# Local attention with a sink: the value products of a turn as four matmuls on tiles that hold a high and a low half side by side, the halves added outside TensorE, and the masks of the own keys made by GpSimd affine selects

## Chip, core, metric

One NeuronCore of a Trainium2 chip runs the kernel. The metric is the device time of one execution in microseconds, as the median of several runs.

## What is computed

Two transformer blocks follow each other on 512 tokens of width 1024. The change touches one part of the second block, the sliding-window attention with a sink: 16 query heads share 2 key heads of width 64, and a query attends to its own 128-token block up to itself and to the part of the block before that lies within the window of 128.

```python
def sliding_window_sink_attention(q, k, v, sinks, valid):
    ...
    kb, vb = band(k), band(v)          # the block before, then the own block
    ...
    mask = ((diff >= 0) & (diff < WINDOW))[None] & kvalid[:, None, :]
    scores = jnp.where(mask[None, :, None, None], scores, -jnp.inf)
    ...
    probs = jax.nn.softmax(jnp.concatenate([scores, sink], axis=-1), axis=-1)[..., :-1]
    o = jnp.einsum('bnhgqk,bnkhd->bnqhgd', probs.astype(v.dtype), vb)
# second_block
y_sw = (o_sw * jax.nn.silu(sw_z)) @ w_branch_swa[l]
```

A query at place t of its block attends to exactly 128 keys: own keys 0 to t and keys t+1 to 127 of the block before. So one 128x128 tile of probabilities for each head holds both kinds.

## The kernel before

Five engines run programs written out by hand, and semaphores order them. Each engine works strictly in its own order. Exact products come from numbers split into a high part (rounded to the type of the fast matmul, `fp32r`) and a low part (the rest): high by high, high by low and low by high are summed in PSUM.

The local attention runs in 16 turns w = 0 to 15, one for four heads of one block of 128 queries. For one turn:

- TensorE (PE) makes the scores (`window_scores`, L2522). VectorE (DVE) lays the own keys over the keys of the block before (L1906), adds the sink and takes the maximum (`window_max`, L1908). ScalarE (ACT) takes the exponentials (`window_exp`, L1201), VectorE the reciprocals of the sums (`window_norm`, L1914), GpSimd (POOL) multiplies by them (`window_normalised`, L718).
- TensorE transposes the probabilities of four heads into one PSUM bank, 128 keys by 512 (`window_transposed`, L2531). ScalarE copies the bank as the high part into `pwt` (`transposed_hi`), VectorE subtracts it and writes the low part (`transposed_lo`, shown under the helper's line L1651).
- The values are the block before plus a step: o = P·V_before + (P masked to the own keys)·(V_own − V_before). The masked copy of the high part is made by VectorE (L1886), that of the low part by GpSimd (`window_own_low`, L710), each as a product with a 0/1 tile.
- TensorE multiplies (`window_values`, L2543 to L2551): six matmuls of 512 columns into PSUM bank 6. The value tiles `before_hi`, `before_lo`, `step_hi`, `step_lo` hold the same 64 columns twice, so that rows 0 to 63 and rows 64 to 127 of the bank hold the same sums; the output of an even head is read from the first, that of an odd head from the second.
- VectorE multiplies the bank by half the gate (`window_out`, L1898, two instructions of 64x256), ScalarE makes the high part of the result (`window_out_hi`), GpSimd the low part (`window_out_lo`, L696).

Around it TensorE interleaves, for each pass w of its loop, the scores of turn w+2, some steps of the gate projections (`merge_gate`, three matmuls a step, under L1982 to L1984), the transposes of turn w, and the values of turn w−1. In passes 15 and 16 a branch product of 12 matmuls stands in the place of the gate steps. GpSimd also makes the low part of two weight slabs in six pieces (`part_low`, L703) in passes 3, 4, 6, 7, 11 and 12; whole slabs before and after are under L632. VectorE makes the low part of slab 21 in pass 14 (L1651). `pwt` is one buffer before the change: ScalarE may not overwrite it before the six matmuls of the last turn have ended (`swo_done`).

Of the kernel before, what the change touches and what calls it, by code (L numbers as in the profile page):

```python
# [12 lines left out]
P = 128  # L13
SEQ, D = 512, 1024
NT, KT = SEQ // P, D // P
HD = 64
# [87 lines left out]
def build(nc, a, out):  # L104
    with ExitStack() as ctx:
# [43 lines left out]
        step_hi = sb("step_hi", [P, NT, 2, 2, HD], F32R, at[0] - 4 * KB)  # L149
# [79 lines left out]
        step_lo = sb("step_lo", [P, NT, 2, 2, HD], F32R)  # L229
        r_tokm = region(4 * KB)  # L230
        before_hi = sb("before_hi", [P, NT, 2, 2, HD], F32R, r_tokm)
# [7 lines left out]
        at[0] = tok_start + 5 * KB  # L239
        before_lo = sb("before_lo", [P, NT, 2, 2, HD], F32R)  # L240
        pwt = sb("pwt", [P, 2, 2, SEQ], F32R)
# [159 lines left out]
        sqp_done = sem("sqp_done")  # L401
# [30 lines left out]
        ymain_done = sem("ymain_done")  # L432
# [14 lines left out]
        sw_exp = sem("sw_exp")  # L447
        pw_ready = sem("pw_ready")
# [124 lines left out]
        def _(pool):  # L573
# [103 lines left out]
            def values_low(lo, v, hi, copy_):  # L677

                return pool.tensor_tensor(lo[:, :, :, copy_, :], v.rearrange("p t (g d) -> p t g d", g=2),
                                          hi[:, :, :, copy_, :].bitcast(F32), ALU.subtract)  # L680

            pool.wait_ge(vw_hi, 1)
            for copy_ in range(2):
                values_low(step_lo, v_step[:], step_hi, copy_).then_inc(vw_lo, 1)
            pool.wait_ge(vw_hi, 2)
            pool.wait_ge(tw_done, 10)
            for copy_ in range(2):
                values_low(before_lo[:, 0:1], insert_dim(v_meta[:], 1, 1), before_hi[:, 0:1], copy_)
                values_low(before_lo[:, 1:], tokw[:, 0:3, 1152:1280], before_hi[:, 1:], copy_).then_inc(vw_lo, 1)
# [17 lines left out]
            def window_own_low(w):  # L707

                pool.wait_ge(tw_lo, 10 + w + 1)
                pool.tensor_tensor(by_head(pwt[:, 1, 1, :]), by_head(pwt[:, 1, 0, :].bitcast(F32)),  # L710
                                   insert_dim(own_keys.bitcast(F32), 1, 4), ALU.mult).then_inc(window_own_lo, 1)
# [11 lines left out]
            for w in range(16):  # L723
                window_own_low(w)
# [32 lines left out]
        def _(act):  # L757
# [386 lines left out]
            def values_high(hi, v):  # L1144

                for copy_ in range(2):
                    last = copy(hi[:, :, :, copy_, :], v.rearrange("p t (g d) -> p t g d", g=2))
                return last

            for half in range(2):  # L1150
                split2(11 + 2 * half)
                if half == 1:
                    act.wait_ge(v_step_ready, 2)
                    values_high(step_hi, v_step[:]).then_inc(vw_hi, 1)
# [30 lines left out]
            act.wait_ge(vw_lo, 2)  # L1185
            values_high(before_hi[:, 0:1], insert_dim(v_meta[:], 1, 1))
            values_high(before_hi[:, 1:], tokw[:, 0:3, 1152:1280]).then_inc(vw_hi, 1)
# [39 lines left out]
            def window_out_hi(w):  # L1227

                n, u = turn_of(w)
                act.wait_ge(swo_read, w + 1)  # L1230
                copy(qw[:, 4 * u:4 * u + 4:2, n * P:n * P + P], yw[:, w % 2]).then_inc(yw_hi, 1)

            merge_tanh(0)
            for w in range(16):
                transposed_hi(w)
                if w == 14:
                    split2(21)
# [8 lines left out]
                if w + 1 in GATE_ENDS:  # L1246
                    merge_tanh(1 + GATE_ENDS.index(w + 1))
            window_out_hi(15)
# [33 lines left out]
        def _(dve):  # L1282
# [1423 lines left out]
```

## Time and profile before

| | us |
|---|---|
| median of 3 runs (966.72 to 967.11) | 966.81 |
| the profiled execution, time | 967.21 |
| the profiled execution, span of the trace | 965.4 |
| PE busy | 948.9 (98%) |
| PEld (weight load) busy | 798.0 (83%) |
| DVE busy | 632.7 (66%) |
| ACT busy | 465.0 (48%) |
| POOL busy | 262.5 (27%) |

The span lies within the time of the execution; the difference is 1.8 us at its ends. Busy shares are those of the whole program; the 16 turns take about 75 us of it.

### The profile page before, as it was taken

The numbers are of one execution on the slowest core, as the hardware profiler recorded it, in microseconds if no ns is written. First come the engines' busy times: TensorE is split into PE (matmuls) and PEld (weight loads), VectorE is DVE, ScalarE is ACT, GpSimd is POOL, SyncE is SP. The second block draws the span as 40 slices with busy tenths as digits, with TensorE's granted clock in tenths as the row PEclk, the third lists the DMA queues.
The fourth block names the chain that finished last, engine by engine and source line by source line (L and its number), as shares of the span: only waits on it lengthen the run. The fifth ranks groups of instructions, "written<-read, shape, count | busy, mean of one in ns | idle before, by whom it ended". The sixth has DMA issues, their size and how long they took to land.

```text
span 965.4 us, 12758 instructions
## 1 busy us (share of the span) xinstructions
PE 948.9 (98%) x4782; PEld 798.0 (83%) x4782; DVE 632.7 (66%) x914; ACT 465.0 (48%) x844; POOL 262.5 (27%) x190
## 2 busy tenths in 40 slices
PE   7999999999999999999999999999999999999997
PEld 6988888888888888888888888988888887888886
DVE  5677787946787687864755887699547775312314
ACT  5435665725444565634447778523555652221212
POOL 2226000003235000002253010151358884315141
PEclk9999999999999999999999999999999999999999
DMA  9232201132422201143222111122220113232312
GB/s 299 90 112 76 96 23 44 44 131 79 144 88 88 93 19 63 45 131 83 88 88 88 43 45 44 45 88 88 87 88 22 45 43 109 88 105 93 131 44 87
DMA packets 64189, 79.84 MB, mean 83 GB/s; under 512 B 5744, under 2 KB 47856, under 8 KB 64128
## 3 DMA queue, kind: packets, MB, share of 16 engines
q1 hardware_dynamic: 62224, 76.13, 24.6%
q10 hardware_dynamic: 1904, 2.88, 0.9%
q8 instruction: 40, 0.66, 0.3%
q14 instruction: 21, 0.17, 0.1%
HBM read 76.91 MB, written 2.10 MB: 82 GB/s over the span
## 4 chain that ended last, share of the span: by engine, by line
PE 41%; issue 40%; POOL 8%; ACT 6%; DVE 4%; DMA 1%; POOLq 0%; ACTq 0%; DVEq 0%
PE ps L1982 12%; PE ps L1983 11%; PE ps L1984 11%; POOL small L604 2%; PE ps L2522 1%; POOL t L614 1%; POOL sq L614 1%; DVE sp L1745 1%; ACT spr L1016 1%; DMA x<-in_x 1%; POOL small L591 1%; DVE wlo L1651 1%; ACT qsb L1016 1%; PE ps L2531 1%; POOL small L593 1%
## 5 line engine op out<-in xcount | busy, mean ns | idle before, releaser
L632 POOL TENSOR_TENSOR wlo<-raw,whi 128x2048 fp32r<-128x2048 f32 (+1 forms) x23 | 101.1, 4395 | 184.8 <-ACT whi L1010 175.4
L1982 PE MATMUL ps<-whi,hhi 128*128 128x512 f32 (+1 forms) x320 | 115.7, 362 | 1.1 <-issue 0.4
L1984 PE MATMUL ps<-whi,hlo 128*128 128x512 f32 (+1 forms) x320 | 114.5, 358 | 0.0
L1983 PE MATMUL ps<-wlo,hhi 128*128 128x512 f32 (+1 forms) x320 | 114.4, 357 | 0.0
L1982 PE MATMUL ps<-hhi,whi 128*128 128x512 f32 x288 | 113.5, 394 | 0.6 <-POOL wlo L703 0.6
L1984 PE MATMUL ps<-hhi,wlo 128*128 128x512 f32 x288 | 112.4, 390 | 0.0
L1983 PE MATMUL ps<-hlo,whi 128*128 128x512 f32 x288 | 112.2, 390 | 0.0
L1010 ACT ACTIVATE whi<-raw 128x2048 fp32r<-128x2048 f32 (+1 forms) x29 | 52.9, 1826 | 84.4 <-PE ps L1984 75.9
L1320 DVE TENSOR_TENSOR wlo<-raw,whi 128x2048 fp32r<-128x2048 f32 (+1 forms) x29 | 63.6, 2192 | 37.4 <-ACT whi L773 30.9
L773 ACT ACTIVATE whi<-raw 128x2048 fp32r<-128x2048 f32 (+1 forms) x29 | 52.1, 1798 | 69.4 <-PE ps L1984 69.4
L2039 PE MATMUL ps<-hhi,whi 128*128 128x512 f32 x192 | 76.8, 400 | 0.0
L2041 PE MATMUL ps<-hhi,wlo 128*128 128x512 f32 x192 | 75.1, 391 | 0.0
L2040 PE MATMUL ps<-hlo,whi 128*128 128x512 f32 x192 | 74.8, 390 | 0.0
L1651 DVE TENSOR_TENSOR wlo<-raw,whi 128x2048 fp32r<-128x2048 f32 x10 | 23.6, 2357 | 72.9 <-ACT whi L1010 72.7
L1982 PEld LDWEIGHTS ps<-whi,hhi 128*128 128x128 f32 x320 | 60.5, 189 | 11.3 <-issue 2.3
L618 POOL TENSOR_TENSOR small<-small 128x4 f32<-128x4 f32 x2 | 0.4, 201 | 253.1 <-ACT junk L971 253.1
L1984 PEld LDWEIGHTS ps<-whi,hlo 128*128 128x128 f32 x320 | 60.5, 189 | 8.9
L1983 PEld LDWEIGHTS ps<-wlo,hhi 128*128 128x128 f32 x320 | 60.5, 189 | 8.3
L1982 PEld LDWEIGHTS ps<-hhi,whi 128*128 128x128 f32 x288 | 54.1, 188 | 11.8 <-POOL wlo L703 0.8
L1984 PEld LDWEIGHTS ps<-hhi,wlo 128*128 128x128 f32 x288 | 54.1, 188 | 11.6
L1983 PEld LDWEIGHTS ps<-hlo,whi 128*128 128x128 f32 x288 | 54.1, 188 | 10.3
L898 ACT ACTIVATE prob<-ps,small 128x512 f32<-128x512 f32 x64 | 43.4, 685 | 25.0 <-DVE small L1525 24.9
(339 smaller groups left out, 2266.2 us busy)
## 6 DMA issues: line engine op xcount, KB each, us to landing
raw<-in_w_in SPq DMA_DIRECT2D x42, 1024.0 KB, 5.3
raw<-in_w_out SPq DMA_DIRECT2D x12, 1024.0 KB, 5.0
raw<-in_w_in SPq DMA_DIRECT2D x10, 512.0 KB, 4.0
raw<-in_w_branch_swa SPq DMA_DIRECT2D x4, 1024.0 KB, 5.0
raw<-in_w_branch_sb SPq DMA_DIRECT2D x4, 512.0 KB, 3.4
x<-in_x ACTq DMA_DIRECT2D x3, 512.0 KB, 6.6
out<-x SPq DMA_DIRECT2D x3, 512.0 KB, 2.6
ws<-in_spatial_w SPq DMA_DIRECT2D x2, 512.0 KB, 6.6
```

The source lines that it names most:

```text
L632: pool.tensor_tensor(wlo[s][:, 0:n, :], raw[s][:, 0:n, :], whi[s][:, 0:n, :].bitcast(F32), ALU.subtract).then_inc(slab_split, 1)
L773: act.activation(whi[s][:, :, 0:w], raw[s][:, :, 0:w], ACT.Copy).then_inc(whi_done, 1)
L898: act.activation(prob[:, t, :], ps[:, n % 3, :], ACT.Exp, bias=nmax[:, m:m + 1], accum_out=pair_sums(psum_e, h // 2)[:, m:m + 1]).then_inc ...
L1010: act.activation(whi[s][:, 0:n, :], raw[s][:, 0:n, :], ACT.Copy).then_inc(whi_done, 1)
L1320: dve.tensor_tensor(wlo[s][:, :, 0:w], raw[s][:, :, 0:w], whi[s][:, :, 0:w].bitcast(F32), ALU.subtract).then_inc(slab_split, 1)
L1651: return dve.tensor_tensor(lo, src, hi.bitcast(F32), ALU.subtract)
L1982: pe.matmul(out_ap, lhsT=lhi(k), rhs=rhi(k), start=first and k == 0, stop=False, skip_group_check=True)
L1983: pe.matmul(out_ap, lhsT=lhi(k), rhs=rlo(k), start=False, stop=False, skip_group_check=True)
L1984: m = pe.matmul(out_ap, lhsT=llo(k), rhs=rhi(k), start=False, stop=last and k == n - 1, skip_group_check=True)
L2039: pe.matmul(ps[:, bank, :], lhsT=wh, rhs=hhi[:, k, :], start=k == 0, stop=False)
L2040: pe.matmul(ps[:, bank, :], lhsT=wh, rhs=hlo[:, k, :], start=False, stop=False)
L2041: m = pe.matmul(ps[:, bank, :], lhsT=wl, rhs=hhi[:, k, :], start=False, stop=k == KT - 1)
```

## The change

The tiles `before` and `step` now hold the high part in columns 0 to 63 and the low part in columns 64 to 127 (for each of the two key heads). One matmul with such a tile gives the product with the high part in PSUM rows 0 to 63 and that with the low part in rows 64 to 127; four matmuls make a turn: `before` and `step`, each with the high and the low part of the probabilities. The two halves of the bank have to be added. For even heads the addend stands in rows 64 to 127, for odd heads in rows 0 to 63: ScalarE copies it across into a tile `other` (`window_other_half`), VectorE adds it to the half that stays, and a third VectorE instruction of 128x256 multiplies by the gate. Both masked copies are now made on GpSimd (`window_own`) by `affine_select`, which takes the element where query − key ≥ 0 and writes zero elsewhere. `pwt` has two buffers. On VectorE the order of `transposed_lo` and `window_out` in a pass is turned round. The preparation of the value tiles writes each part once, not twice.

```diff
-        pwt = sb("pwt", [P, 2, 2, SEQ], F32R)
+        other = sb("other", [P, 2, P])
+        pwt = sb("pwt", [P, 2, 2, 2, SEQ], F32R)
...
+            def window_own(w, part):
+
+                pool.wait_ge((tw_hi, tw_lo)[part], 10 + w + 1)
+                place = lambda own: by_head(pwt[:, w % 2, part, own, :])
+                pool.affine_select(place(1), place(0).bitcast(F32), [[0, 4], [1, P]], ALU.is_ge, 0.0, base=0,
+                                   channel_multiplier=-1).then_inc((window_own_hi, window_own_lo)[part], 1)
...
             for w in range(16):
-                window_own_low(w)
+                window_own(w, 0)
+                window_own(w, 1)
...
             def transposed_hi(w):
                 act.wait_ge(tw_done, 10 + w + 1)
+                if w >= 2:
+                    act.wait_ge(swo_done, w - 1)
+                copy(pwt[:, w % 2, 0, 0, :], ps[:, 4 + w % 2, :]).then_inc(tw_hi, 1)
+
+            def window_other_half(w):
+
+                act.wait_ge(swo_done, w + 1)
                 if w:
-                    act.wait_ge(swo_done, w)
-                copy(pwt[:, 0, 0, :], ps[:, 4 + w % 2, :]).then_inc(tw_hi, 1)
+                    act.wait_ge(swo_read, w)
+                for e in range(2):
+                    r, o = slice(64 * e, 64 * e + 64), slice(64 - 64 * e, P - 64 * e)
+                    last = copy(other[r], ps[o, 6, :].rearrange("p (c e n) -> p c e n", c=2, e=2)[:, :, e, :])
+                last.then_inc(other_done, 1)
...
             for w in range(16):
                 transposed_hi(w)
+                if w:
+                    window_other_half(w - 1)
...
             def transposed_lo(w):
 
                 dve.wait_ge(tw_hi, 10 + w + 1)
-                low(pwt[:, 1, 0, :], ps[:, 4 + w % 2, :], pwt[:, 0, 0, :]).then_inc(tw_lo, 1)
-                dve.tensor_tensor(by_head(pwt[:, 0, 1, :]), by_head(pwt[:, 0, 0, :].bitcast(F32)),
-                                  insert_dim(own_keys.bitcast(F32), 1, 4), ALU.mult).then_inc(window_own_hi, 1)
+                p = pwt[:, w % 2]
+                low(p[:, 1, 0, :], ps[:, 4 + w % 2, :], p[:, 0, 0, :]).then_inc(tw_lo, 1)
...
-                    last = dve.scalar_tensor_tensor(yw[r, w % 2], o, 0.5, gate_sw[r, 2 * u:2 * u + 2, n * P:n * P + P],
-                                                    ALU.mult, ALU.mult)
+                    last = dve.tensor_tensor(yw[r, w % 2], o, other[r], ALU.add)
                 last.then_inc(swo_read, 1)
+                dve.wait_ge(swo_read, w + 1)
+                dve.scalar_tensor_tensor(yw[:, w % 2], yw[:, w % 2], 0.5, gate_sw[:, 2 * u:2 * u + 2, n * P:n * P + P],
+                                         ALU.mult, ALU.mult).then_inc(window_gated, 1)
...
-                pe.matmul(ps[:, 6, :], lhsT=v(before_hi), rhs=pwt[:, 0, 0, :], start=True, stop=False)
-                pe.matmul(ps[:, 6, :], lhsT=v(before_lo), rhs=pwt[:, 0, 0, :], start=False, stop=False)
+                pe.matmul(ps[:, 6, :], lhsT=v(before), rhs=p[:, 0, 0, :], start=True, stop=False)
                 pe.wait_ge(tw_lo, 10 + w + 1)
-                pe.matmul(ps[:, 6, :], lhsT=v(before_hi), rhs=pwt[:, 1, 0, :], start=False, stop=False)
+                pe.matmul(ps[:, 6, :], lhsT=v(before), rhs=p[:, 1, 0, :], start=False, stop=False)
                 pe.wait_ge(window_own_hi, w + 1)
-                pe.matmul(ps[:, 6, :], lhsT=v(step_hi), rhs=pwt[:, 0, 1, :], start=False, stop=False)
-                pe.matmul(ps[:, 6, :], lhsT=v(step_lo), rhs=pwt[:, 0, 1, :], start=False, stop=False)
+                pe.matmul(ps[:, 6, :], lhsT=v(step), rhs=p[:, 0, 1, :], start=False, stop=False)
                 pe.wait_ge(window_own_lo, w + 1)
-                pe.matmul(ps[:, 6, :], lhsT=v(step_hi), rhs=pwt[:, 1, 1, :], start=False, stop=True).then_inc(swo_done, 1)
+                pe.matmul(ps[:, 6, :], lhsT=v(step), rhs=p[:, 1, 1, :], start=False, stop=True).then_inc(swo_done, 1)
```

GpSimd's order at the start of the turns, before. The first row is the low part of slab 18, and the rows on `pwt` are the masked low parts of turns 0, 1 and 2.

```order
L632 TENSOR_TENSOR wlo_55<-raw_51,whi_53 128x2048 [waits whi_done]
L710 TENSOR_TENSOR pwt<-pwt,consts_r 128x512 [waits tw_lo]
L718 TENSOR_TENSOR pw<-pw,small_99 128x4x128 [waits inv_ready]
L710 TENSOR_TENSOR pwt<-pwt,consts_r 128x512 [waits tw_lo]
L696 TENSOR_TENSOR qw<-yw,qw 128x2x128 [waits yw_hi]
```

The same place after the change (its line numbers are the changed file's: L629 is the slab's low part, L706 `window_own`, L714 `window_normalised`, L691 `window_out_lo`).

```order
L629 TENSOR_TENSOR wlo_55<-raw_51,whi_53 128x2048 [waits whi_done]
L706 ISA
L706 AFFINE_SELECT pwt<-pwt 128x512 [waits tw_hi]
L706 AFFINE_SELECT pwt<-pwt 128x512 [waits tw_lo]
L714 TENSOR_TENSOR pw<-pw,small_99 128x4x128 [waits inv_ready]
L706 AFFINE_SELECT pwt<-pwt 128x512 [waits tw_hi]
L706 AFFINE_SELECT pwt<-pwt 128x512 [waits tw_lo]
L691 TENSOR_TENSOR qw<-yw,qw 128x2x128 [waits yw_hi]
```

VectorE's order in one turn, before: low part, masked high part, `window_max`, `window_norm`, and then the output of the turn.

```order
L1651 TENSOR_TENSOR pwt<-ps,pwt 128x512 [waits tw_hi]
L1886 TENSOR_TENSOR pwt<-pwt,consts_r 128x512
L1906 COPY_PREDICATED ps<-consts_r,ps 128x4x128 [waits sw_scored]
L1907 COPY ps<-sink 128x4 [waits dch]
L1908 TENSOR_REDUCE small_99<-ps 128x4 [waits dch]
L1914 RECIPROCAL small_99<-small_99 128x4 [waits sw_exp]
L1898 SCALAR_TENSOR_TENSOR yw<-ps,gate_sw 64x256 [waits swo_done]
L1898 SCALAR_TENSOR_TENSOR yw<-ps,gate_sw 64x256
```

After (L1659 is the low part, L1905 the addition of the halves, L1908 the gating):

```order
L1659 TENSOR_TENSOR pwt<-ps,pwt 128x512 [waits tw_hi]
L1905 TENSOR_TENSOR yw<-ps,other 64x256 [waits other_done]
L1905 TENSOR_TENSOR yw<-ps,other 64x256
L1908 SCALAR_TENSOR_TENSOR yw<-yw,gate_sw 128x256 [waits swo_read]
L1915 COPY_PREDICATED ps<-consts_r,ps 128x4x128 [waits sw_scored]
```

The masked high part is gone from VectorE, a gating instruction of its own has come, and the output of a turn now stands between the low part and `window_max`.

## Rows read from the trace of the kernel before

**Rows 1.** busy time by stretches: PE, PEld, DVE, ACT, POOL, then clock, DMA

```profile
729.00:802.00 73.00, 72.04 (x392) 60.51 (x391) 56.98 (x117) 39.98 (x146) 60.32 (x51) 1.00 0.14 44
...
850.00:900.00 50.00, 50.00 (x222) 41.43 (x221) 8.93 (x11) 11.73 (x13) 14.46 (x4) 1.00 0.32 102
```

**Rows 2.** waits of TensorE from 730 us on: us, times, longest

```profile
PE ps L1982 <- POOL wlo L703: 0.6, 1, 0.6
PE ps L2551 <- POOL pwt L710: 0.4, 1, 0.4
```

**Rows 3.** TensorE in order of time, values of turn 1: start, length

```profile
734.25 0.60 PE L2531 MATMUL ps<-ident,pw 128*128 128x128 f32 x4
734.61 0.48 PE L2543 MATMUL ps<-pwt,before_hi 128*128 128x512 f32 x1
734.92 0.40 PE L2544 MATMUL ps<-pwt,before_lo 128*128 128x512 f32 x1
...
735.85 0.39 PE L2551 MATMUL ps<-pwt,step_hi 128*128 128x512 f32 x1
```

**Rows 4.** GpSimd by line and shape: busy us, mean ns, idle before

```profile
L710 POOL TENSOR_TENSOR pwt<-pwt,consts_r 128x512 fp32r<-128x512 f32 x16 | 26.9, 1682 | 11.7 <-DVE pwt L1651 11.7
L718 POOL TENSOR_TENSOR pw<-pw,small 128x512 f32<-128x512 f32 x16 | 16.6, 1040 | 1.0 <-DVE small L1914 1.0
L696 POOL TENSOR_TENSOR qw<-yw,qw 128x256 fp32r<-128x256 f32 x16 | 13.8, 861 | 1.3 <-ACT qw L1016 1.3
L703 POOL TENSOR_TENSOR wlo<-raw,whi 128x512 fp32r<-128x512 f32 x6 | 7.7, 1288 | 0.0
L649 POOL CAST whi<-raw 128x2048 fp32r<-128x2048 f32 x4 | 7.6, 1900 | 70.8 <-DVE spr L1651 70.8
```

**Rows 5.** GpSimd and VectorE in order of time, turns 0 and 1

```profile
723.87 4.61 POOL L632 TENSOR_TENSOR wlo<-raw,whi 128x2048 fp32r<-128x2048 f32 x1 [0.55 <-ACT whi L1010]
727.85 1.19 DVE L1886 TENSOR_TENSOR pwt<-pwt,consts_r 128x512 fp32r<-128x512 f32 x1
728.44 1.74 POOL L710 TENSOR_TENSOR pwt<-pwt,consts_r 128x512 fp32r<-128x512 f32 x1
...
732.93 0.68 DVE L1886 TENSOR_TENSOR pwt<-pwt,consts_r 128x512 fp32r<-128x512 f32 x1
733.10 1.67 POOL L710 TENSOR_TENSOR pwt<-pwt,consts_r 128x512 fp32r<-128x512 f32 x1 [1.32 <-DVE pwt L1651]
```

**Rows 6.** VectorE by line and shape, 715 to 805 us

```profile
L1898 DVE SCALAR_TENSOR_TENSOR yw<-ps,gate_sw 64x256 f32<-64x256 f32 x32 | 13.5, 422 | 14.3 <-PE ps L2551 14.0
L1886 DVE TENSOR_TENSOR pwt<-pwt,consts_r 128x512 fp32r<-128x512 f32 x16 | 12.6, 790 | 0.0
L1908 DVE TENSOR_REDUCE small<-ps 128x4 f32<-128x516 f32 x16 | 11.1, 695 | 0.5
L1651 DVE TENSOR_TENSOR pwt<-ps,pwt 128x512 fp32r<-128x512 f32 x16 | 11.1, 692 | 1.4 <-ACT pwt L1016 0.9
```

**Rows 7.** ScalarE by line, then waits, 710 to 810 us

```profile
L1016 ACT ACTIVATE qw<-yw 128x256 fp32r<-128x256 f32 x16 | 6.9, 430 | 4.8 <-DVE yw L1898 4.6
...
ACT pwt L1016 <- PE ps L2551: 26.0, 15, 2.9
POOL pwt L710 <- DVE pwt L1651: 11.7, 13, 1.6
```

**Rows 8.** TensorE, VectorE and GpSimd in order of time, last turns

```profile
791.62 0.49 PE L2551 MATMUL ps<-pwt,step_hi 128*128 128x512 f32 x1
794.64 2.98 DVE L1651 TENSOR_TENSOR wlo<-raw,whi 128x2048 fp32r<-128x2048 f32 x1 [0.32 <-ACT whi L1010]
795.43 2.78 POOL L696 TENSOR_TENSOR qw<-yw,qw 128x256 fp32r<-128x256 f32 x1
```

**Rows 9.** GpSimd in order of time, the first microseconds

```profile
0.85 0.10 POOL L576 MEMSET small<- 128x8 f32 x1
5.56 0.19 POOL L582 TENSOR_TENSOR small<-small 128x1 f32<-128x1 f32 x1 [4.60 <-ACT junk L797]
```

More of the change, by code:

```diff
@@ L228, in build @@
         gate_sw = sb("gate_sw", [P, 8, SEQ])
-        step_lo = sb("step_lo", [P, NT, 2, 2, HD], F32R)
         r_tokm = region(4 * KB)
-        before_hi = sb("before_hi", [P, NT, 2, 2, HD], F32R, r_tokm)
+        before = sb("before", [P, NT, 2, 2, HD], F32R, r_tokm)
         tokm = sb("tokm", [META, 1, 256], F32, r_tokm)
@@ L676, in _, with values_low @@
                         .then_inc(v_step_ready, 1)
-            def values_low(lo, v, hi, copy_):
-                return pool.tensor_tensor(lo[:, :, :, copy_, :], v.rearrange("p t (g d) -> p t g d", g=2),
-                                          hi[:, :, :, copy_, :].bitcast(F32), ALU.subtract)
+            def values_low(tile, v):
+                return pool.tensor_tensor(tile[:, :, :, 1, :], v.rearrange("p t (g d) -> p t g d", g=2),
+                                          tile[:, :, :, 0, :].bitcast(F32), ALU.subtract)
             pool.wait_ge(vw_hi, 1)
-            for copy_ in range(2):
-                values_low(step_lo, v_step[:], step_hi, copy_).then_inc(vw_lo, 1)
+            values_low(step, v_step[:]).then_inc(vw_lo, 1)
             pool.wait_ge(vw_hi, 2)
             pool.wait_ge(tw_done, 10)
-            for copy_ in range(2):
-                values_low(before_lo[:, 0:1], insert_dim(v_meta[:], 1, 1), before_hi[:, 0:1], copy_)
-                values_low(before_lo[:, 1:], tokw[:, 0:3, 1152:1280], before_hi[:, 1:], copy_).then_inc(vw_lo, 1)
+            values_low(before[:, 0:1], insert_dim(v_meta[:], 1, 1))
+            values_low(before[:, 1:], tokw[:, 0:3, 1152:1280]).then_inc(vw_lo, 1)
             def window_out_lo(w):
@@ L1144, in values_high @@
             def values_high(hi, v):
-                for copy_ in range(2):
-                    last = copy(hi[:, :, :, copy_, :], v.rearrange("p t (g d) -> p t g d", g=2))
-                return last
+                return copy(hi[:, :, :, 0, :], v.rearrange("p t (g d) -> p t g d", g=2))
             for half in range(2):
@@ L1184, in _ @@
             act.wait_ge(rope2_done, 5)
-            act.wait_ge(vw_lo, 2)
-            values_high(before_hi[:, 0:1], insert_dim(v_meta[:], 1, 1))
-            values_high(before_hi[:, 1:], tokw[:, 0:3, 1152:1280]).then_inc(vw_hi, 1)
+            act.wait_ge(vw_lo, 1)
+            values_high(before[:, 0:1], insert_dim(v_meta[:], 1, 1))
+            values_high(before[:, 1:], tokw[:, 0:3, 1152:1280]).then_inc(vw_hi, 1)
             def transposed_hi(w):
                 act.wait_ge(tw_done, 10 + w + 1)
-                if w:
-                    act.wait_ge(swo_done, w)
-                copy(pwt[:, 0, 0, :], ps[:, 4 + w % 2, :]).then_inc(tw_hi, 1)
+                if w >= 2:
[3 more added lines that the diff above has]
+                act.wait_ge(swo_done, w + 1)
+                if w:
+                    act.wait_ge(swo_read, w)
[3 more added lines that the diff above has]
+                last.then_inc(other_done, 1)
             def window_exp(w):
@@ L1229, in window_out_hi @@
                 n, u = turn_of(w)
-                act.wait_ge(swo_read, w + 1)
+                act.wait_ge(window_gated, w + 1)
                 copy(qw[:, 4 * u:4 * u + 4:2, n * P:n * P + P], yw[:, w % 2]).then_inc(yw_hi, 1)
@@ L1921, in _ @@
             for w in range(16):
+                transposed_lo(w)
                 if w:
                     window_out(w - 1)
-                transposed_lo(w)
                 if w == 14:
```

19 lines of the change are left out of this document (7 added, 12 removed).

## Prediction

> **What bounds the kernel now.** I read the page's table of engines first: TensorE is busy for 98% of the span, and since matmuls overlap there, I went on to what it waits for. From 730 us to the end it waits twice, 0.6 and 0.4 us, both times for GpSimd [rows 2]; the stretches behind the turns show it busy without a gap [rows 1]. So a microsecond that TensorE saves in the turns arrives at the end, and so does one that it loses. In the turns the other engines are not far behind: of 73 us GpSimd is busy for 60.3 and VectorE for 57.0, ScalarE for 40.0 [rows 1]. GpSimd's 60.3 already is 83%, and the change gives it work while it shortens the time in which the work must be done. That is the question of this case.
>
> **What TensorE saves.** In a row of value products the starts are (735.85 − 734.92) / 4 = 0.23 us apart [rows 3]; the first takes 0.31 and stays. Two of six go in each turn: 2 × 0.23 × 16 = 7.4 us, the most that can be gained.
>
> **What VectorE and ScalarE get.** VectorE loses the masked copy (0.79 mean, 0.68 undisturbed) and gains a gating of 256 columns; its nearest row is the old output instruction with as many columns, 0.42 [rows 5, 6]. The two additions cost what the two old instructions did. So VectorE gets shorter by 0.26 a turn, unless it is held (next part). ScalarE gets two copies of 64x256; a copy of 128x256 takes 0.43 [rows 7], so at most 0.86 a turn. It waited 26.0 us in 15 turns for the last matmul of the turn before, because `pwt` was one buffer [rows 7]; that wait goes, and the copies, which wait for the same matmul, take its place. Queued behind them are `window_exp` and, on VectorE behind the additions, `window_max` (0.70 for its reduction [rows 6]), whose scores TensorE made a whole pass earlier. I cost this at nothing on the path; if that cover were gone, it would be the 0.86 × 16 = 14 us of the copies at worst. The preparation of the value tiles gets shorter on ScalarE and GpSimd, but ahead of the turns GpSimd next waits for others, at last for the slab whose low part starts at 723.87 with 0.55 us of idle time ahead of it [rows 5]: nothing gained.
>
> **What GpSimd gets.** Here a hold has to be read first. VectorE's masked copy reads two tiles of SBUF. The one at 727.85 takes 1.19 instead of 0.68: GpSimd's slab runs until 728.48, and the copy ends at 729.04. GpSimd's next, begun 728.44, ends at 730.18, 1.14 us after that. The one at 733.10 takes 1.67, and VectorE's copy runs until 733.61: again 1.16 of its own [rows 5]. In the last turns a VectorE subtraction of two SBUF tiles takes 2.98 and a GpSimd one beside it 2.78, where 0.86 is that line's mean [rows 4, 8]. So while one of the two engines runs such an instruction, the other is held until its end. The Trainium skill says this too (GPSIMD Engine Reference, Specifications: shared SBUF interfaces, contention with VectorE instructions that have two SBUF inputs); the rows agree. The masked copy held GpSimd for about 0.5 a turn; that goes. The new gating reads `yw` and `gate_sw`, both SBUF, so it holds GpSimd for 0.42, and waits itself for what GpSimd is doing.
>
> Let a be the time of one select. Until TensorE's last value matmul of turn 13, GpSimd must finish, from 728.48 on: 14 pairs of selects (28a), 12 low parts of the output at 0.73 (the line's 13.8 us less the 2.78, over 15), 13 normalisations at 1.04, 6 slab pieces at 1.29, and 13 holds of 0.42 [rows 4, 6, 8]: 28a + 8.8 + 13.5 + 7.7 + 5.5 = 28a + 35.5. I add 2 us, an estimate for idle time in the first turns, where it has not fallen behind (before it waited 11.7 in 13 turns [rows 7]). TensorE came to that matmul at 791.62 [rows 8]; without 14 × 0.46 = 6.4 us it would be there at 785.2, which leaves GpSimd 56.7 us. It is late from a = (56.7 − 37.5) / 28 = 0.69 on, and each 0.1 us more costs 2.8 us.
>
> No row shows a select. From below: the cast, one operand, takes 1.90 for 2048 columns, which is 0.48 for 512 [rows 4]. From above: the product that makes the same masked tile with two operands, 1.67 as it stands, 1.15 without the hold [rows 4, 5]. Nothing excludes more than that, since a select must also make its condition for each element. I take 0.95, nearer to the product, whose tile and four rows of 128 it shares. Then GpSimd needs 26.6 + 37.5 = 64.1, and TensorE waits 64.1 − 56.7 = 7.4 us, at the third and fourth value matmul: all of the saving.
>
> The Trainium skill prices single-input instructions on GpSimd as roughly at line rate (GPSIMD Engine Reference, When to use GPSIMD), which would be 512 cycles at 1.2 GHz, an estimate of 0.43 us, and so no lateness; the same page (Performance versus the Vector engine) puts branching on data at about 12 cycles an element, 5.1 us here. The sum goes by neither.
>
> **The `ISA` row.** The reload of the library stands between the slab and the first select, with TensorE's values of turn 0 due 1.3 us later. Its like at the start ran in an idle stretch of 4.60 us that ended when ScalarE's result came [rows 9], so it takes between 0 and 4.6. Since nothing shows that it filled the stretch, I take 1.2. The skill puts the first call after loading code at about 6 us (GPSIMD Engine Reference, Instruction dispatch); the 4.60 of the stretch is less, so here the rows and the page differ.
>
> **The last turns.** In turns 14 and 15 VectorE's 2.98 us now stands ahead of `transposed_lo` of turn 15, and two selects instead of one product follow; TensorE already waited 0.4 there [rows 2, 8]. An estimate from these rows: 1.0 more.
>
> **Sum**: −7.4 + 7.4 + 1.2 + 1.0 = +2.2 us. On the profiled execution 967.21 + 2.2 = 969.4; the median shown is 0.4 below that execution, so 969.0.
>
> **The rivals.**
> 1. Forecast: the select takes 0.8 to 1.15, the reload little. GpSimd becomes the bound of the turns. With 0.8: −7.4 + 3.2 + 2.2 = −2.0; with 1.15: −7.4 + 13.0 + 2.2 = +7.8. Its own range is 965 to 975. Chance 0.37.
> 2. Faster: the select is near the cast, 0.5 to 0.75. At 0.54 GpSimd needs 15.1 + 37.5 = 52.6, under 56.7. A turn with a slab piece takes it 1.08 + 0.73 + 1.04 + 1.29 + 0.42 = 4.6, more than TensorE's, so about 1 us stays, and 0.5 for the reload: −7.4 + 1.5 = −5.9, 960.9. It decides the sign at a = (56.7 + 7.4 − 2.2 − 37.5) / 28 = 0.87. For it speaks that only one operand is read. Chance 0.28.
> 3. The reload is dear: 3 to 4.6 us, during which TensorE stands in turn 0, at a select of 0.8: −2.0 − 1.2 + 4 = +0.8, at 0.95 +5.0; 967.6 to 972. For it: an instruction in front of the first select that nothing needed before. Against it: the same library is loaded already. Chance 0.20.
> 4. The select is dearer than the product. At 1.67: 46.8 + 37.5 − 56.7 = 27.6, less 7.4, and 2.2: +22.4, 989. The skill's branching rule would make it 28 × 5.1 + 37.5 − 56.7 = 124 of waiting; the slow end of this case, a chance of 0.02 within it. Chance 0.15.
>
> **Numbers.** A measurement of this kernel tells about 0.2%, 1.9 us, from no change. Faster: most of rival 2 (0.26) and the lower end of the forecast (0.05). Same: 0.13 of the forecast, 0.05 of rival 3, 0.02 of rival 2: 0.20. Slower: the rest, 0.49. Range for 8 in 10: from rival 2's 961 to 982, which is a select of 1.45; beyond it lie the faster tip of rival 2 and most of rival 4.
>
> **What the profile after would show.** Right: 64 matmuls of values; the selects near 0.95 without a hold; GpSimd nearly without idle time from 729 to 785; TensorE waiting at the values for the selects, some 7 us in all; the gating on VectorE longer than 0.42 where it meets GpSimd. Wrong: selects of 0.6 and a GpSimd that still waits for VectorE (rival 2); a gap of several us ahead of the first select only (rival 3); or TensorE waiting for `other` or `swo_read`, which I cost at nothing.

## The result and the profile after

The changed kernel takes 960.38 us (median of 4 runs, 960.18 to 960.69) where the kernel before takes 966.76 beside it: a ratio of 0.9932, interval 0.9921 to 0.9944. It is faster by 6.4 us, 0.66%. The forecast of 969.0 had the wrong sign and the time lies below its range; the time is close to the second rival's 960.9, the one with a cheap select. The profiled execution took 960.69 us, against 967.21 before: 6.5 less.

GpSimd by line and shape, 715 to 806 us, in the changed kernel (busy us, mean ns, idle time before; to be laid beside [rows 4]):

```profile
L706 POOL TENSOR_SCALAR_AFFINE_SELECT pwt<-pwt 128x512 fp32r<-128x512 f32 x32 | 21.2, 684 | 0.1
L714 POOL TENSOR_TENSOR pw<-pw,small 128x512 f32<-128x512 f32 x16 | 16.7, 1044 | 4.3 <-DVE small L1923 4.1
L691 POOL TENSOR_TENSOR qw<-yw,qw 128x256 fp32r<-128x256 f32 x16 | 13.5, 846 | 12.1 <-ACT qw L1013 12.1
L698 POOL TENSOR_TENSOR wlo<-raw,whi 128x512 fp32r<-128x512 f32 x6 | 7.7, 1289 | 0.0
```

32 selects take 21.2 us, where 16 products took 26.9. GpSimd is idle for some 16 us in this window, waiting for ScalarE's copy (12.1) and VectorE's inverse (4.1). The same engine in order of time: the selects of turns 0, 2 and 3, then of 12, 14 and 15:

```profile
724.03 4.61 POOL L629 TENSOR_TENSOR wlo<-raw,whi 128x2048 fp32r<-128x2048 f32 x1 [0.55 <-ACT whi L1007]
728.67 1.23 POOL L706 TENSOR_SCALAR_AFFINE_SELECT pwt<-pwt 128x512 fp32r<-128x512 f32 x2
...
736.06 1.22 POOL L706 TENSOR_SCALAR_AFFINE_SELECT pwt<-pwt 128x512 fp32r<-128x512 f32 x2
...
740.43 1.41 POOL L706 TENSOR_SCALAR_AFFINE_SELECT pwt<-pwt 128x512 fp32r<-128x512 f32 x2
...
779.48 1.29 POOL L698 TENSOR_TENSOR wlo<-raw,whi 128x512 fp32r<-128x512 f32 x1
780.73 1.41 POOL L706 TENSOR_SCALAR_AFFINE_SELECT pwt<-pwt 128x512 fp32r<-128x512 f32 x2
...
788.19 1.22 POOL L706 TENSOR_SCALAR_AFFINE_SELECT pwt<-pwt 128x512 fp32r<-128x512 f32 x2
790.23 2.54 POOL L691 TENSOR_TENSOR qw<-yw,qw 128x256 fp32r<-128x256 f32 x1 [0.81 <-ACT qw L1013]
792.72 1.22 POOL L706 TENSOR_SCALAR_AFFINE_SELECT pwt<-pwt 128x512 fp32r<-128x512 f32 x2
```

A pair of selects takes 1.22, so one takes 0.61; where VectorE's gating meets the pair, it takes 1.41. The reload of the library stands between 724.03 + 4.61 = 728.64 and 728.67: a gap of 0.03 us, where the product before began 0.04 us ahead of its slab's end [rows 5].

The waits of TensorE and its weight load from 729 us on (us in total, times, longest), beside [rows 2]:

```profile
PEld ps L1991 <- POOL wlo L698: 1.3, 1, 1.3
...
PE ps L1991 <- POOL wlo L698: 1.1, 1, 1.1
PEld ps L2559 <- POOL pwt L706: 1.0, 3, 0.4
PEld ps L2557 <- POOL pwt L706: 0.7, 1, 0.7
...
PE ps L2557 <- POOL pwt L706: 0.3, 1, 0.3
```

And TensorE in order of time: the values of turns 0, 12 and 15 (the last):

```profile
729.91 0.48 PE L2553 MATMUL ps<-pwt,before 128*128 128x512 f32 x1
...
730.69 0.39 PE L2559 MATMUL ps<-pwt,step 128*128 128x512 f32 x1
...
780.94 0.39 PE L2555 MATMUL ps<-pwt,before 128*128 128x512 f32 x1
781.60 0.51 PE L2557 MATMUL ps<-pwt,step 128*128 128x512 f32 x1 [0.28 <-POOL pwt L706]
782.19 0.50 PE L2559 MATMUL ps<-pwt,step 128*128 128x512 f32 x1
...
794.58 0.39 PE L2559 MATMUL ps<-pwt,step 128*128 128x512 f32 x1
```

In turn 12 the last three values start 0.66 and 0.59 apart instead of 0.23: 0.8 us lost behind two selects that came late. That is the second wait of the changed kernel, the first being 1.1 for the slab's last low part. The last value of turn 15 starts at 800.90 before and at 794.58 after:

```profile
800.13 0.40 PE L2549 MATMUL ps<-pwt,step_lo 128*128 128x512 f32 x1
800.90 0.50 PE L2551 MATMUL ps<-pwt,step_hi 128*128 128x512 f32 x1 [0.37 <-POOL pwt L710]
```

(of the kernel before, the same view). The difference of 6.32 can be added up from starts. From the first value of turn 0 (729.77 before, 729.91 after) to the last of turn 15 the kernel before takes 71.13 and the changed one 64.67, 6.46 less; 0.14 goes because turn 0 begins later. In 11 of the 15 steps from a turn's first value to the next turn's the changed kernel is shorter by 0.44 to 0.47, 5.06 in all: that is the two matmuls. The rest, in us:

| stretch | before | after | gained | what stands in it |
|---|---|---|---|---|
| turn 7 to turn 8 | 5.01 | 5.01 | 0.00 | the wait for the slab's last low part, 0.6 before, 1.1 after |
| turn 12 to turn 13 | 4.83 | 5.01 | −0.18 | after: 0.78 lost behind late selects |
| turn 13 to turn 14 | 4.65 | 4.38 | 0.27 | after: 0.17 lost at the last value |
| turn 14 to turn 15 | 4.19 | 3.78 | 0.41 | |
| turn 15, first to last value | 1.68 | 0.78 | 0.90 | before: a gap of 0.77 ahead of the very last value |

5.06 + 0.00 − 0.18 + 0.27 + 0.41 + 0.90 = 6.46. Without its wait the step from turn 7 to turn 8 takes 3.71 in the kernel with earlier pieces below, so the wait costs the changed kernel 1.30; with the selects alone it takes 4.30, so it cost the kernel before 0.71. Behind the last value nothing changes: 164.5 us to the end of the trace before, 164.4 after.

Both waits name GpSimd, but the chain of work that ended last (the profile's critical chain, start and length in us) begins further back. For the slab's last part, and then for the late selects of turn 12:

```profile
752.21 0.38 ACT other L1013
...
752.61 1.51 ACT pw L1206 x8
...
761.40 1.23 POOL wlo L698
```

```profile
774.86 0.39 ACT other L1013
...
776.16 0.51 DVE yw L1908
...
779.52 1.25 POOL wlo L698
```

The first goes from the last value of turn 5 through ScalarE's copy of the other half, the exponentials, a piece of the slab's high part and `window_out_hi`, to GpSimd, which then has no gap until the slab's last low part at 761.40. The second goes from the last value of turn 10 through that copy, the additions, the gating and `window_max` to GpSimd's normalisation, the slab piece and the selects. So the copies, which the change adds to ScalarE, are on the path at both places, and the additions at the second.

### The profile page after: what moved, and what is told of

Same layout as the page of the kernel before. It is cut to its first block, busy times and chain, and to the rows that moved or that the text cites. A ratio compares the mean times of both kernels' runs of the same rounds, so it can differ in the third digit from the quotient of the medians.

```text
span 959.0 us, 12753 instructions
## 1 busy us (share of the span) xinstructions
PE 941.1 (98%) x4750; PEld 791.2 (83%) x4750; DVE 629.9 (66%) x914; ACT 477.2 (50%) x873; POOL 253.4 (26%) x203
## 4 chain that ended last, share of the span: by engine, by line
issue 40%; PE 40%; POOL 8%; ACT 5%; DVE 4%; DMA 1%; POOLq 0%; ACTq 0%; DVEq 0%
PE ps L1991 12%; PE ps L1993 11%; PE ps L1992 11%; POOL small L601 2%; DMA x<-in_x 1%; PE ps L2531 1%; POOL t L611 1%; POOL sq L611 1%; DVE sp L1753 1%; ACT spr L1013 1%; POOL small L588 1%; ACT qsb L1013 1%; DVE wlo L1659 1%; PE ps L2267 1%; ACT sp L1077 1%
## 5 line engine op out<-in xcount | busy, mean ns | idle before, releaser
L629 POOL TENSOR_TENSOR wlo<-raw,whi 128x2048 fp32r<-128x2048 f32 (+1 forms) x23 | 101.1, 4396 | 183.5 <-ACT whi L1007 174.1
L1659 DVE TENSOR_TENSOR wlo<-raw,whi 128x2048 fp32r<-128x2048 f32 x10 | 22.9, 2287 | 72.8 <-ACT whi L1007 72.5
```

The costliest lines, as they stand in the source:

```text
L629: pool.tensor_tensor(wlo[s][:, 0:n, :], raw[s][:, 0:n, :], whi[s][:, 0:n, :].bitcast(F32), ALU.subtract).then_inc(slab_split, 1)
L1659: return dve.tensor_tensor(lo, src, hi.bitcast(F32), ALU.subtract)
```

## The experiments

Each was measured beside the kernel before, whose medians in the three sets of runs were 967.13, 966.94 and 966.90 us.

**What the two matmuls bring.** The second value product is issued three times, so that there are six again (the same product added twice more; the output is another).

```
-                pe.matmul(ps[:, 6, :], lhsT=v(before), rhs=p[:, 1, 0, :], start=False, stop=False)
+                for _ in range(3):
+                    pe.matmul(ps[:, 6, :], lhsT=v(before), rhs=p[:, 1, 0, :], start=False, stop=False)
```

> The changed kernel with the second value matmul (before x low part) issued three times, so that a turn has six matmuls again; the output is not the reference's. Theory A, the gain is TensorE's two matmuls a turn and nothing else: 32 x 0.23 = 7.4 us come back, less some waiting for GpSimd that they hide, 966 to 968 us. Rival B, the gain is from the second buffer of the probabilities and from lighter work on VectorE: the time stays under 963.

966.27 us, ratio 0.9992 (0.9983 to 1.0002). Theory A: with six matmuls everything else that the change does comes to no difference that can be told. The 5.9 us to the changed kernel are the matmuls: 7.4 less what TensorE then waits for selects, which it didn't here (its one wait is 1.0 for the slab).

**The masks as products.**

```
-                pool.affine_select(place(1), place(0).bitcast(F32), [[0, 4], [1, P]], ALU.is_ge, 0.0, base=0,
-                                   channel_multiplier=-1).then_inc((window_own_hi, window_own_lo)[part], 1)
+                pool.tensor_tensor(place(1), place(0).bitcast(F32), insert_dim(own_keys.bitcast(F32), 1, 4),
+                                   ALU.mult).then_inc((window_own_hi, window_own_lo)[part], 1)
```

> The changed kernel with both masked copies on GpSimd as products with the 0/1 tile, in the place of the selects. Theory A, the forecast's account of GpSimd is right and only the price of the select was off: at 1.15 us for a product GpSimd needs 28 x 1.15 + 37.5 = 69.7 us where TensorE leaves it 56.7, so 13 us of waiting come on top of the changed kernel's 960.4, 973. Rival B, GpSimd has room that the account does not see: 965 or less.

971.93 us, ratio 1.0052 (1.0035 to 1.0069), 1 us under Theory A's 973. GpSimd by line, 715 to 806 us, then TensorE's waits from 700 us on:

```profile
L706 POOL TENSOR_TENSOR pwt<-pwt,consts_r 128x512 fp32r<-128x512 f32 x32 | 43.0, 1364 | 0.0
```

```profile
PE ps L2559 <- POOL pwt L706: 6.0, 9, 0.9
PE ps L1991 <- POOL wlo L698: 1.5, 1, 1.5
PE ps L2557 <- POOL pwt L706: 1.4, 3, 0.7
PE ps L2553 <- DVE yw L1905: 0.5, 1, 0.5
```

This is the profile that the prediction described (GpSimd without idle time before its masks, TensorE waiting some 7 us for them at the third and fourth value) at twice the select's price: what it said of this mechanism is right, and some 11 us hang on the kind of instruction alone.

**The masks where they were**: the high part's product on VectorE, the low part's on GpSimd, the rest as changed.

```
+                dve.tensor_tensor(by_head(p[:, 0, 1, :]), by_head(p[:, 0, 0, :].bitcast(F32)),
+                                  insert_dim(own_keys.bitcast(F32), 1, 4), ALU.mult).then_inc(window_own_hi, 1)
...
-                window_own(w, 0)
                 window_own(w, 1)
```

> The changed kernel with the masks made as before the change: the high part as a product on VectorE, the low part as a product on GpSimd. Theory A, VectorE would become the bound: its turn is 0.61 + 0.61 + 0.89 + 0.45 + 1.54 + 0.20 = 4.3 us where TensorE's mean turn is 4.07, and each product there and the gating meet GpSimd's holds: 965 to 970, slower than the changed kernel by 5 or more. Rival B, the four matmuls gain without the selects: 960 to 962.

969.51 us (968.21 to 970.48), ratio 1.0025 (1.0014 to 1.0036): Theory A. The two matmuls, bought with the halves, are worth nothing if the masks stay. In the traced execution, one of the fastest (968.28), TensorE waits 3.2 us for the product on GpSimd, 2.0 for VectorE's additions and 1.9 for the slab, and GpSimd's low parts of the slab are held (mean 1.73 instead of 1.29). The eight executions fall into two groups by the mean clock that TensorE was granted: 968.21 to 968.42 at 0.999 of the full clock, and 969.42 to 970.48 at 0.996 or 0.997. So some 1.2 us of the 2.4 that the median lies above the kernel before go with a lower clock. Masks as products don't pay in either place; whether one product on VectorE beside one select on GpSimd would, was not run.

**One buffer for the turned weights.**

```
-                if w >= 2:
-                    act.wait_ge(swo_done, w - 1)
-                copy(pwt[:, w % 2, 0, 0, :], ps[:, 4 + w % 2, :]).then_inc(tw_hi, 1)
+                if w:
+                    act.wait_ge(swo_done, w)
+                copy(pwt[:, 0, 0, 0, :], ps[:, 4 + w % 2, :]).then_inc(tw_hi, 1)
...
```

> The changed kernel with a single buffer of the transposed probabilities, so that ScalarE waits for the last matmul of the turn before, as before the change. Theory A, the two buffers hide a part: masks start about 0.9 us later in a turn, and TensorE waits in the turns with slab pieces, 1 to 2 us in all, 961.5 to 962.5. Rival B, the buffer is what makes the gain: 965 or more.

963.59 us (963.40 to 965.01), ratio 0.9967 (0.9953 to 0.9982): 3.2 above the changed kernel, between the theories. The traced execution is a slow one of the five, 964.64. In it ScalarE's wait for the last value is back (13.8 us in 14 turns), and TensorE waits 0.8 + 0.2 for selects, 0.5 for the additions and 1.6 for the slab. Behind that last wait it also loses its clock. Busy times from 764 to 766 us (the third number from the right is the granted clock), then a matmul of the gate:

```profile
764.00:766.00 2.00, 2.00 (x6) 1.47 (x5) 1.90 (x5) 0.94 (x4) 1.63 (x3) 0.50 0.61 185
```

```profile
764.76 0.63 PE L1991 MATMUL ps<-hhi,whi 128*128 128x512 f32 x1
```

The granted clock is 0.50 from 764 to 767 us (1.2 GHz, the lower of its two levels), and the next matmul starts 0.42 later instead of 0.23. From the end of the wait to the first value of turn 8 it takes 3.16 where the changed kernel takes 1.85, and another 0.29 is lost by turn 9: 1.6 us by the clock, of the 3.95 that this execution lies above the traced one of the changed kernel. The changed kernel's wait of 1.1 us at the same place left the clock at 1.00, and so did one of 1.9 in the traced kernel with the masks as before.

**One select more in each turn**, into a tile that nobody reads:

```
+                if part == 0:
+                    pool.wait_ge(spare_done, w)
+                    pool.affine_select(by_head(spare[:]), place(0).bitcast(F32), [[0, 4], [1, P]], ALU.is_ge, 0.0, base=0,
+                                       channel_multiplier=-1).then_inc(spare_done, 1)
```

> The changed kernel, with one select more in each turn: the high part's select is made twice, first into a tile that nobody reads. GpSimd gets 16 x 0.61 = 9.8 us of work more. It asks what headroom GpSimd has, that is from what price of a select on TensorE would be late. Theory A (the account of the prediction with the select as measured): GpSimd must finish 42 selects and 35.5 us of other work in the 56.7 us up to turn 13, and 42 x 0.61 + 35.5 + 2 = 63.1, so TensorE waits about 6 us more at the third and fourth value matmul: 966 to 967. Theory B (the account's other terms are too high, since the selects hardly hold VectorE and are hardly held by it; GpSimd was idle for some 16 us in the changed kernel's turns): most of the 9.8 us goes into idle time and TensorE waits only 1 to 4 us more: 961.5 to 964.5. Theory C (GpSimd far from the path): under 961.

964.31 us (963.92 to 965.96), ratio 0.9975 (0.9965 to 0.9986): Theory B, near its upper edge.

**Every select twice**, the same lines for both parts:

> The changed kernel with every select made twice, first into a tile that nobody reads, which prices a select at 2 x 0.61 = 1.22 us. This is the upper end of the prediction's first case. Theory A (the account of the prediction): 28 x 1.22 + 37.5 = 71.7 against 56.7 us, so TensorE waits 15 us: 975. Theory B (the account's other terms are some 4 to 5 us too high): the slope of 28 us for each us of price stands once GpSimd has no idle time left, and the time is 969 to 972, that is, from the one extra select of the kernel before it another 7 to 8.5 us, all of it as TensorE's waiting for selects. If instead the second extra select costs under 5 us, GpSimd is still not the bound of the turns even at 1.22.

970.68 us (969.63 to 971.52), ratio 1.0039 (1.0024 to 1.0054): the time is Theory B's, but it lies 6.4 us above the kernel with one extra, less than the 7 to 8.5 expected. One turn of GpSimd in it, in order of time:

```profile
743.65 0.74 POOL L693 TENSOR_TENSOR qw<-yw,qw 128x256 fp32r<-128x256 f32 x1
744.35 1.05 POOL L719 TENSOR_TENSOR pw<-pw,small 128x512 f32<-128x512 f32 x1
745.35 1.30 POOL L700 TENSOR_TENSOR wlo<-raw,whi 128x512 fp32r<-128x512 f32 x1
746.59 0.83 POOL L709 TENSOR_SCALAR_AFFINE_SELECT spare<-pwt 128x512 fp32r<-128x512 f32 x1
747.38 0.63 POOL L711 TENSOR_SCALAR_AFFINE_SELECT pwt<-pwt 128x512 fp32r<-128x512 f32 x1
747.97 0.63 POOL L709 TENSOR_SCALAR_AFFINE_SELECT spare<-pwt 128x512 fp32r<-128x512 f32 x1
748.55 0.63 POOL L711 TENSOR_SCALAR_AFFINE_SELECT pwt<-pwt 128x512 fp32r<-128x512 f32 x1
749.16 0.73 POOL L693 TENSOR_TENSOR qw<-yw,qw 128x256 fp32r<-128x256 f32 x1
```

From start to start the turn takes 749.16 − 743.65 = 5.51. By the prediction's prices it would be 0.73 + 1.04 + 1.29 + 0.42 + 4 × 0.61 = 5.92. Two things make it shorter: each instruction starts 0.02 to 0.06 before the row of the one ahead ends (seven times, 0.30 in all), and the hold costs the held select 0.2 (0.83 against 0.63), not the gating's 0.42; against them the lengths themselves are 0.11 above the prices. Together 0.41. Over 13 turns, some of them without a slab piece, that is 4 to 5 us, about what the account's 975 was above the measured 970.7.

**The selects without the rest**: the kernel before, both masks as selects, VectorE's masked copy gone, six matmuls and one buffer.

```
...
+                for part in range(2):
+                    pool.wait_ge((tw_hi, tw_lo)[part], 10 + w + 1)
+                    pool.affine_select(by_head(pwt[:, part, 1, :]), by_head(pwt[:, part, 0, :].bitcast(F32)), ...)
...
-                dve.tensor_tensor(by_head(pwt[:, 0, 1, :]), by_head(pwt[:, 0, 0, :].bitcast(F32)),
-                                  insert_dim(own_keys.bitcast(F32), 1, 4), ALU.mult).then_inc(window_own_hi, 1)
```

> The kernel before with one part of the change: both masked copies made as selects on GpSimd, VectorE's masked copy gone; six value matmuls, one pwt and the old output instructions stay. Theory A (TensorE was hardly waiting for masks, 1.0 us in all the turns of the kernel before, so moving them gains at most that): 965.8 to 967.2, no change that can be told. Theory B (the masks were what bounded the turns of the kernel before, by the chain from the transposes through VectorE's masked copy to the values): 962 to 964.5, and then part of the gain is the masks' and not that of the two matmuls.

965.34 us, ratio 0.9983 (0.9974 to 0.9992): 1.6 us faster, 0.5 below Theory A's band and 0.8 above Theory B's. TensorE waits for nothing from 700 to 800 us; what went are the waits of [rows 2], with the weight load's share of them: 0.71 ahead of turn 8, 0.39 in turns 12 and 13, and 0.54 ahead of the very last value. So the selects are worth more than the 1.0 us of waits that TensorE's own rows show.

**The slab's pieces a turn earlier.**

```
-GATE_SLAB_HI, GATE_SLAB_LOW = [3, 4, 6, 7], [4, 5, 7, 8]
+GATE_SLAB_HI, GATE_SLAB_LOW = [3, 4, 5, 6], [4, 5, 6, 7]
```

> The changed kernel with another place for the pieces of the output gate's slab: ScalarE's high parts at turns 3, 4, 5, 6 instead of 3, 4, 6, 7 and GpSimd's low parts at 4, 5, 6, 7 instead of 4, 5, 7, 8. The first scores-sized matmul of the gate on this slab waits 1.1 us for the last low part at 762.7 us, plus some at the weight load. Theory A (the piece simply comes a turn late): the wait goes and nothing is late in its place, 958.8 to 959.6. Theory B (GpSimd has four turns with a piece in a row, each 4.3 to 4.6 us against TensorE's 4.1, so its selects fall behind): TensorE waits for the selects in turns 6 and 7 instead, 960 to 961.5.

958.94 us, ratio 0.9917 (0.9904 to 0.9931). Once more, with the changed kernel on the same chip:

> The changed kernel as it is, once more, on the same chip as the two variants that follow: 960.2 to 960.7 as before. It is the measure for them.

> The kernel with the slab's pieces a turn earlier, beside the changed kernel on the same chip. Theory A (the 1.1 us wait for the last low piece is gone and was on the path): 1.1 to 1.7 us under the changed kernel beside it. Theory B (the 958.94 measured before was the chip's): less than 0.5 us under it.

960.67 (960.33 to 960.75) and 959.10 us (958.99 to 959.51). The runs don't overlap: 1.6 us faster than the changed kernel, Theory A. TensorE's only wait there is 0.3, at L2557 in turn 12; four full turns in a row are no trouble, since GpSimd has slack right before and behind them (0.55 and 0.60 us of idle time) and takes 4.44 us for such a turn, where TensorE's take 4.29 on average there, too little to fall behind by in four turns.

**The next slab's pieces apart.**

```
-BRANCH_HI, BRANCH_LOW = [9, 10], [12, 13]
+BRANCH_HI, BRANCH_LOW = [9, 10], [10, 12]
```

> The kernel with the early pieces, and GpSimd's two low pieces of the next slab at turns 10 and 12 instead of 12 and 13, so that they no longer stand in two turns one behind the other, where TensorE waited 0.3 us for a select and its weight load 0.7. Theory A (that wait was GpSimd's lateness in two full turns): it goes, 958.3 to 958.8. Theory B (one full turn is enough to make a select late, since the piece stands right ahead of it): 958.8 to 959.3, the wait only moves.

959.03 us (958.70 to 959.36), beside 959.10 without it: no difference. TensorE in it, in order of time, turn 12:

```profile
779.64 0.39 PE L2555 MATMUL ps<-pwt,before 128*128 128x512 f32 x1
780.38 0.50 PE L2557 MATMUL ps<-pwt,step 128*128 128x512 f32 x1 [0.35 <-POOL pwt L706]
780.97 0.51 PE L2559 MATMUL ps<-pwt,step 128*128 128x512 f32 x1
```

The late select is still the one of turn 12, though the turn before it and the turn after it now are without a piece. Theory B: one full turn is enough. The piece stands right ahead of its selects, and the critical chain above shows the rest of what makes them late: the copies and additions of turn 10.

**ScalarE's copies twice**, each first into a tile that nobody reads.

```
...
+                    act.wait_ge(spare_done, 2 * w + e)
+                    copy(spare[r], ps[o, 6, :].rearrange("p (c e n) -> p c e n", c=2, e=2)[:, :, e, :])\
+                        .then_inc(spare_done, 1)
                     last = copy(other[r], ps[o, 6, :].rearrange("p (c e n) -> p c e n", c=2, e=2)[:, :, e, :])
```

> The changed kernel with ScalarE's two copies of 64x256 made twice in each turn, each first into a tile that nobody reads: 16 x 0.77 = 12.3 us of ScalarE more, in the chain from the last value matmul of a turn through the copies and the additions to the gating and the next turn's row maxima. It tests the step of the prediction that costed these copies at nothing. Theory A (the chain runs beside a whole pass of TensorE and has a turn of slack, so the copies are covered twice over): 960.2 to 961.5. Theory B (ScalarE's copy of the high part of the transposes stands behind them and already waits for the last value matmul; VectorE already waits for ScalarE's copies 6.0 and 4.9 us): TensorE waits at the transposed halves in each turn, up to 12 us more, and at least 3: 963 to 972.

963.35 us, ratio 0.9963 (0.9950 to 0.9976). Of 12.1 us more on ScalarE 2.7 arrive, nearly a quarter. ScalarE by line and VectorE's wait for it, 715 to 800 us:

```profile
L1015 ACT ACTIVATE spare<-ps 64x256 f32<-64x256 f32 x32 | 12.1, 379 | 3.6 <-PE ps L2564 3.1
```

```profile
DVE yw L1910 <- ACT other L1015: 11.4, 14, 2.1
```

The time is at Theory B's lower edge, far from its 12 us and clear of Theory A. TensorE waits at other places than Theory B said: 1.5 for the slab, 0.8 for a select and 0.4 for the additions. So most of a copy is covered, and what isn't shows mostly as GpSimd's lateness.

## Why the prediction was wrong

**The step that failed is the price of a select**: 0.95 taken, nearer to the product, "whose tile and four rows of 128 it shares"; measured 0.61. The cast with one operand, the lower bound at 0.48, was the nearer neighbour: both read one SBUF operand, and the product, 1.36 in the same place, reads two. These rows fit a price by the number of operands; they don't show that nothing else counts (0.13 lie between cast and select, and none of the runs varies the condition). The Trainium skill's rule that single-input instructions run roughly at line rate (GPSIMD Engine Reference, When to use GPSIMD), from which the prediction made an estimate of 0.43, was nearer to the row than 0.95. The Trainium skill's about 12 cycles an element for branching on data (GPSIMD Engine Reference, Performance versus the Vector engine), an estimate of 5.1 us in the prediction, is not what this instruction takes.

**The account of GpSimd's time was dear as well.** Price of a select, with what each would bring over the kernel before beside it:

| one select, us | kernel | time, us | against before, us |
|---|---|---|---|
| 0.61 | changed | 960.67 | −6.2 |
| 0.92 | one more in a turn | 964.31 | −2.6 |
| 1.22 | each twice | 970.68 | +3.7 |

Between the last two rows the line meets the kernel before at 0.92 + 0.30 × 2.6 / 6.4 = 1.04, an estimate. The prediction put that point at 0.87. With a select of 0.95 this kernel would by the same line have come out near 965, faster by 1.9 us. So the sign was wrong for two reasons: the price, and some 4 us too much in the other terms. Where these lie can be read at a price of 1.22, from the trace of the kernel with each select twice:

```profile
793.93 0.51 PE L2564 MATMUL ps<-pwt,step 128*128 128x512 f32 x1 [0.68 <-POOL pwt L711]
...
803.99 0.40 PE L2564 MATMUL ps<-pwt,step 128*128 128x512 f32 x1
```

The account gives 28 × 1.22 + 37.5 − 56.7 = 15.0 of waiting and a sum of −7.4 + 15.0 + 2.2 = +9.8; the last value of turn 15 starts 803.99 − 800.90 = 3.1 later than before, 6.7 less. Most of that is there at the last value of turn 13, which starts at 793.93 where the account has 785.2 + 15.0 = 800.2: 6.3. The holds make 13 × 0.22 = 2.9 of it (0.42 taken, 0.2 measured), and lengths added up where starts lie about 0.04 closer make 3.5 (87 instructions; the forecast's own kernel has 59 of them, 2.4). The reload makes 1.1 more (below), and the last turns take 0.7 back: at this price they cost 1.7, not 1.0. Against all this stands what a sum over 14 turns can't see, that single turns are late before the sum is: 0.8 in turn 12 of the changed kernel, where the account at 0.61 has no waiting.

**The reload**: 1.2 taken, 0.07 measured (the gap of 0.03 against a start 0.04 ahead of the slab's end). The idle stretch of 4.60 at the start [rows 9] said nothing of it, and the third rival falls. The Trainium skill's about 6 us for the first call of a freshly loaded kernel (GPSIMD Engine Reference, Instruction dispatch) isn't seen in this place, where the library was in use already.

**The last turns**: +1.0 taken, −0.4 measured. From the last value of turn 13 to that of turn 15 the kernel before takes 9.28, which is 8.36 without four matmuls, and the changed kernel 7.99 (from 786.59 to 794.58). VectorE's slab did come ahead of turn 15's low half, and GpSimd's `qw` beside it took 2.54, but the selects began at 792.72 and were through in time for the third value at 794.35; two selects of 1.22 together are shorter than the one product of [rows 4], 1.68. With each select twice it is as the prediction feared: a select of turn 14 meets VectorE's slab and takes 2.68, and TensorE waits 1.9 for it.

**The copies and additions, costed at nothing, are on the path.** TensorE never waits for `other` or `swo_read` by name, and most of the 0.77 us a turn is covered. But both waits that the changed kernel has left hang on chains through them (752.21 and 774.86 above), and doubling the copies costs 2.7 of 12.1 us. The cover was called 14 us at worst; it is thinner than that, since it is GpSimd's next instruction that comes late, not TensorE's.

**What was right**: 0.23 us a matmul, of which all 7.4 can be found in TensorE's starts; the direction of each hold; that VectorE's gating takes 0.42 (0.43 undisturbed). For "1 us stays" in full turns the second rival had the right size: 0.8 in turn 12. That its 960.9 is so near is in part luck: it has 0.5 for a reload that takes 0.07, and nothing for the slab's later low part and for the last turns, which nearly cancel. The double buffer was counted only as the end of a wait; without it the kernel is 3.2 us slower. By its own account the upper end of the range was a little off: a select of 1.45 gives +16.2, 983 and not 982.

**The parts do not add up one by one.** Over the kernel before, the selects alone bring 1.6, everything but the two matmuls 0.9 (within the noise), and everything but the selects costs 2.4, about half of it with a lower clock; the whole brings 6.4. The matmuls are the gain, and selects and second buffer are what lets it arrive.

**Open**: how much of the 3.2 us for one buffer is clock in the executions that have no trace; why the clock fell behind one wait for the slab and not behind others as long; whether the number of operands alone sets the price of an instruction on GpSimd; and whether the last piece could be taken out of turn 12 for the 0.8 us there.

## What to carry to other kernels

When no row shows an instruction, try the forecast at the price of each neighbour before choosing one: here the sign hung on it, and the neighbour with the same number of SBUF operands was nearer than the one with the same shape and purpose. When an engine's demand is added up against a deadline, take start to start from the rows instead of lengths; 0.04 us at each of 59 instructions is 2.4 us. When a wait names an engine, follow the critical chain back before calling the work behind it covered. Removing work from a busy engine pays only as far as its suppliers keep up, so look first for the piece that is late next: here moving two pieces of one slab a turn earlier gave another 1.6 us.

## What the runs showed of the hardware

- GpSimd's affine select of 128x512 from SBUF to SBUF takes 0.61 us, a product of the same shape 1.36 in these turns, holds included, a cast 0.48 for as many columns (a quarter of the 1.90 for 2048) [rows 4].
- Selects and VectorE's two-operand gating lock each other out too. VectorE in the changed kernel, in order of time:

```profile
740.88 0.46 DVE L1908 SCALAR_TENSOR_TENSOR yw<-yw,gate_sw 128x256 f32<-128x256 f32 x1
...
779.84 1.21 DVE L1908 SCALAR_TENSOR_TENSOR yw<-yw,gate_sw 128x256 f32<-128x256 f32 x1
...
788.82 0.86 DVE L1908 SCALAR_TENSOR_TENSOR yw<-yw,gate_sw 128x256 f32<-128x256 f32 x1
```

The one at 779.84 begins inside the slab piece of 779.48 and ends 0.32 after the next GpSimd instruction starts; the one at 788.82 begins just after the second select of its pair and ends 0.3 after that select. The one at 740.88 meets the border of two selects (740.43 + 0.61) and is hardly longer, and the pair is 0.19 longer. So a held gating ends 0.3 us after what held it, where an undisturbed one takes 0.43, and a gating that comes first costs the other side 0.2. Selects hold VectorE little here (the gating's mean is 0.58); with each made twice, and GpSimd without idle time, it is 0.83.
- Reloading the library that is in use costs GpSimd under 0.1 us (728.64 to 728.67).
- TensorE's granted clock can fall to 0.50 behind a wait: in one execution with one buffer, after 1.6 us of waiting for the slab, for some 3 us, at a cost of 1.6 us. Other waits of 1.1 to 1.9 us at the same place left it at 1.00.
